# Startup of a one-core diffusion layer: tokens loaded first, the attention modulation in four parts of two k-tiles

## The chip, the cores and the metric

The kernel runs on one core of one Trainium2 chip. The metric is device microseconds of one launch; the median of three runs of the kernel before is 1153.03 us (1152.22 to 1153.11).

## The reference, cut to what matters

The program computes one transformer layer for 512 latent tokens (`x_sample`) and 128 context tokens (`x_prompt`), width 1024, in fp32. The change touches only how it begins:

```python
mod_ctx = (jax.nn.silu(c_ctx) @ w_mod[l] + b_mod[l])[None, None, :]
mod_lat = (jax.nn.silu(c) @ w_mod[l] + b_mod[l])[:, None, :]
...
shift1, scale1, gate1, shift2, scale2, gate2 = jnp.split(mod, 6, axis=-1)
h = rms_norm(x, g_attn) * (1.0 + scale1) + shift1
m, own_ctx = token_mixing(h, mix_w, rope, ctx, lam_init)   # begins with h @ w_in
```

`shift1` and `scale1` are the first 2048 of the 6144 columns of `w_mod` (1024 x 6144). The product `h @ w_in` cannot start before some rows of `h` (transposed: k-tiles of 128 channels) are modulated, and the k-tile k needs columns 128k to 128k+127 of both shift and scale. After it come the two attentions, the output projection and the expert layer of 16 experts, which take the other 1080 us and are not touched.

## The kernel before, in words

The program is written engine by engine, with semaphores; each engine runs its own list in the order in which it is written.

**Loads.** SyncE (SP) issues the weight stream. `STREAM` lists chunks of 1 MB (128 partitions x 2048 floats) and `LOADS` the order of their loads. The first eight chunks, `("part", p, q)`, hold shift and scale columns of the attention modulation: half p of the columns (four k-tiles of shift, four of scale), rows 2q and 2q+1 of the eight k-blocks. Then come the chunks of the dense products, `("gemm", j, q)`. Chunks go round a ring of `NRAW` = 4 buffers `raw`, and a load waits until the chunk four places earlier has been used (`s_half`). The first dense chunk, `FIRST`, has a buffer of its own, `raw_first`, and is loaded between the two halves. After the first part chunk SP also loads `tab` (identity and constants, 100 KB) and five token tiles `x_n` (512 KB each). ScalarE's (ACT's) queue loads the six small rows of `vec` (c, c_ctx, norms, b_mod). GpSimd (POOL) loads `tab2` (rope tables and selectors, 452 KB) at the start, and when part chunk (1, 1) has landed the first key cache, the four lambda rows and two norm rows spread over the partitions (`s_bc`), and the value caches.

**Start.** TensorE (PE) transposes `vec` (L866) after ACT's silu (L1270), and VectorE (DVE) copies it to `vec_t` (L1612). For each token tile, ACT squares and sums it (L1282), POOL takes one over the root (L2232, L2235), DVE scales it (L1654), PE transposes it in 8 pieces (`turn_tokens`, L828), and ACT and DVE copy the two halves out to `x_t` (L1275, L1658). `part_chunk(p, q)` (L807) is four matmuls with 2 stationary columns (c and c_ctx). When a half is complete DVE copies it (`copy_row`, L1620), PE turns it into columns (`part_turn`, L817), and DVE adds the bias (L1625) and forms the scale (L1634). `spin(n)` (L872) is n matmuls of the identity with itself, whose result nobody reads; six more of that kind (L890) follow the first turn.

**First dense product.** `first_step(k)` (L927 to L929) multiplies k-tile k with 512 columns for the five token tiles in banks 0 to 4, three matmuls each: both operands are split into a rounded part (`w_hi`, `ht` high, by ACT, L537 and L1292/L1294) and a rest (`raw_lo`, `ht` low, by DVE, L542 and L1688). Steps 0 to 5 are `first_step`; k-tiles 6 and 7 are the end of `product(0, ...)` (L775 to L777). Between the steps stand the part chunks of half 1 and its turn. Then PE turns the first cached keys (`turn_keys`, L906, copied out by ACT, L1308) and starts `product(1, ...)`. The squares of the first product (L1323) wait in ACT's list behind two splits and an exponential of the lambdas, which wait for DVE.

## Time and profile before

| | |
|---|---|
| median of 3 runs | 1153.03 us |
| profiled execution, first to last instruction (span) | 1148.9 us |
| its own time | not listed apart; the three runs stand 3.3 to 4.2 us above its span |
| PE busy | 1099.2 us (96%) |
| PE's first instruction | 8.67 us |
| first dense matmul | 30.31 us |
| last matmul of the first dense product | 64.7 us |

The span is the time between the first and the last instruction of one profiled execution; what lies around it is launch and completion, so a change of the span is carried over to the median as it is. A busy PE is not a PE at its peak: matmuls are pipelined, and the busy time of a group contains the time that it ran slowly.

### The profile page before, as it was taken

The page shows a single profiled execution, that of the slowest core. Times are in us where ns is not written, and L with a number is a line of the kernel's source. Part 1 is how long each engine was busy: PE and PEld are TensorE (multiplying, and loading weights), DVE is VectorE, ACT ScalarE, POOL GpSimd, SP SyncE. Part 2 cuts the span into 40 slices and gives each one's busy share as a digit, 9 for nine tenths or more (in the row PEclk, how much of TensorE's full clock was granted, in tenths as well). Part 3 has the DMA queues.
Part 4 walks back from the last instruction along what each step waited for, and adds up shares of the span by engine and source line. Part 5 has one row for each costly group of instructions (what it writes and reads, how often), then busy time and mean ns, then how long its engine had stood idle before and what let it go on. Part 6 is the DMA issues. An engine that isn't in the chain of part 4 may idle for free.

```text
span 1148.9 us, 28297 instructions
## 1 busy us (share of the span) xinstructions
PE 1099.2 (96%) x12561; PEld 835.7 (73%) x12561; DVE 543.8 (47%) x993; ACT 369.2 (32%) x856; POOL 154.4 (13%) x213
## 2 busy tenths in 40 slices
PE   6999998999999999999998999999999999999983
PEld 4679887777877777777878777777777777777662
DVE  3575458889968232325877133332233222333235
ACT  4343236777754123122162321222222222211103
POOL 1342440000000000002012111111111111110020
PEclk9999999999999999999999999999999999999996
DMA  9952232212052543368989999999999999999993
GB/s 359 306 224 73 74 74 58 44 25 47 1 198 73 184 146 102 119 220 285 322 301 365 371 403 406 406 406 411 413 407 406 408 406 408 405 408 408 407 322 135
DMA packets 87467, 302.53 MB, mean 263 GB/s; under 512 B 27329, under 2 KB 28610, under 8 KB 62258
## 3 DMA queue, kind: packets, MB, share of 16 engines
q1 hardware_dynamic: 79680, 273.38, 62.0%
q0 software_dynamic: 6528, 20.10, 6.1%
q10 hardware_dynamic: 1138, 7.25, 1.7%
q8 instruction: 99, 1.62, 0.6%
q14 instruction: 22, 0.18, 0.0%
HBM read 276.86 MB, written 18.60 MB: 257 GB/s over the span
## 4 chain that ended last, share of the span: by engine, by line
PE 80%; DVE 6%; DMA 6%; issue 3%; ACT 3%; ACTq 0%; SPq 0%; POOLq 0%; POOL 0%; DVEq 0%
PE ps L1194 39%; PE ps L775 9%; PE ps L777 9%; PE ps L776 9%; PE ps L1001 3%; PE ps L985 2%; DVE neg_max L1794 2%; DMA x_dram<-y_row,rows_t 2%; PE ps L1024 1%; PE ps L1020 1%; DMA x_dram<-xn_p 1%; DVE q_lo_t L1786 1%; PE ps L797 1%; DMA raw<-in_w_in_dram 1%; DMA x_f<-x_dram 1%
## 5 line engine op out<-in xcount | busy, mean ns | idle before, releaser
L2122 DVE SCALAR_TENSOR_TENSOR y_row<-ps,gates,gate_q 32x256 f32<-32x256 f32 (+1 forms) x184 | 88.3, 480 | 237.4 <-PE ps L1194 234.9
L1549 ACT ACTIVATE h_t<-ps 128x256 f32<-128x256 f32 x48 | 15.0, 384 | 371.7 <-PE ps L1194 371.7
L775 PE MATMUL ps<-w_hi,ht 128*128 128x512 f32 (+1 forms) x320 | 124.8, 390 | 0.0
L777 PE MATMUL ps<-w_hi,ht 128*128 128x512 f32 (+1 forms) x320 | 121.8, 381 | 0.0
L776 PE MATMUL ps<-raw_lo,ht 128*128 128x512 f32 (+1 forms) x320 | 121.7, 380 | 0.0
L1194 PE MATMUL ps<-late,xe 128*32 128x256 f32 x1824 | 100.3, 379 | 0.0
L542 DVE TENSOR_TENSOR raw_lo<-raw,w_hi 128x1024 fp32r<-128x1024 f32 x48 | 57.7, 1225 | 78.5 <-ACT w_hi L537 78.0
L1194 PEld LDWEIGHTS ps<-late,xe 128*32 128x32 f32 x1824 | 71.9, 110 | 26.5
L2379 POOL DMA_INDIRECT xg<-x_dram,rows x48 | 46.1, 960 | 318.7 <-PE ps L1194 290.5
L537 ACT ACTIVATE w_hi<-raw 128x1024 fp32r<-128x1024 f32 x48 | 48.8, 1052 | 122.3 <-DMA raw<-in_w_in_dram 67.5
L1539 ACT ACTIVATE xe<-xt,mods_q 128x64 f32<-128x64 f32 x240 | 78.0, 423 | 7.6 <-DVE gates L2106 7.6
L1194 PE MATMUL ps<-raw,xe 128*32 128x256 f32 x1392 | 80.0, 379 | 0.0
L775 PEld LDWEIGHTS ps<-w_hi,ht 128*128 128x128 f32 x320 | 60.1, 188 | 16.6 <-issue 5.2
L1194 PE MATMUL ps<-raw_gate,xe 128*32 128x256 f32 x1248 | 71.3, 379 | 0.0
L1194 PEld LDWEIGHTS ps<-raw,xe 128*32 128x32 f32 x1392 | 54.9, 110 | 20.2
L777 PEld LDWEIGHTS ps<-w_hi,ht 128*128 128x128 f32 x320 | 60.0, 188 | 12.8
L1194 PE MATMUL ps<-late,ht 128*32 128x256 f32 x1200 | 67.5, 379 | 1.1 <-issue 1.1
L776 PEld LDWEIGHTS ps<-raw_lo,ht 128*128 128x128 f32 x320 | 60.2, 188 | 11.3
L1194 PEld LDWEIGHTS ps<-raw_gate,xe 128*32 128x32 f32 x1248 | 49.2, 110 | 18.2
L2113 DVE TENSOR_TENSOR h_t<-h_t,ps 128x256 f32<-128x256 f32 x48 | 19.0, 395 | 88.7 <-PE ps L1194 88.7
L1194 PEld LDWEIGHTS ps<-late,ht 128*32 128x32 f32 x1200 | 47.2, 110 | 18.9 <-issue 1.5
L1794 DVE TENSOR_REDUCE neg_max<-ps 128x1 f32<-128x768 f32 x64 | 58.2, 950 | 2.5 <-PE ps L985 2.4
(325 smaller groups left out, 1916.5 us busy)
## 6 DMA issues: line engine op xcount, KB each, us to landing
late<-in_w_exp_down_dram SPq DMA_DIRECT2D x25, 1024.0 KB, 25.6
late<-in_w_exp_up_dram SPq DMA_DIRECT2D x21, 1024.0 KB, 21.4
late<-in_w_exp_gate_dram SPq DMA_DIRECT2D x17, 1024.0 KB, 23.8
raw<-in_w_in_dram SPq DMA_DIRECT2D x16, 1024.0 KB, 5.8
raw<-in_w_exp_gate_dram SPq DMA_DIRECT2D x16, 1024.0 KB, 23.1
raw_gate<-in_w_exp_up_dram SPq DMA_DIRECT2D x14, 1024.0 KB, 26.4
raw<-in_w_exp_up_dram SPq DMA_DIRECT2D x13, 1024.0 KB, 28.0
raw_gate<-in_w_exp_down_dram SPq DMA_DIRECT2D x13, 1024.0 KB, 24.2
```

The source lines that it names most:

```text
L537: act.activation(w_hi[:, n % NHL, :], raw_half(raw, h), ACT.Copy).then_inc(s_hi, 1)
L542: dve.tensor_tensor(raw_half(raw_lo, h), raw_half(raw, h), w_hi[:, n % NHL, :].bitcast(F32), ALU.subtract)\
L775: pe.matmul(b, stat_hi(k, tt), hi[:, kk, :], start=first, stop=False)
L776: pe.matmul(b, stat_hi(k, tt), lo[:, kk, :], start=False, stop=False)
L777: mm = pe.matmul(b, stat_lo(k, tt), hi[:, kk, :], start=False, stop=last)
L985: mm = pe.matmul(bank(bb, 0, n), q[:, m % 4, t * P:(t + 1) * P], keys_t[:, x, c0:c0 + n], start=(part == 0), stop=(part == 1))
L1001: mm = pe.transpose(bank(4 + n % 3, b * P, (b + 1) * P), prob_row(2 * i + x // per)[:, kt * P:(kt + 1) * P], ident)
L1194: mm = pe.matmul(out[32 * q:32 * q + 32, :], x[:, k, :], columns_of(w, q), start=(k == 0), stop=(k == KD - 1))
L1539: a = act.activation(xe[:, n % 2, sets, k, :], xt[:, sets, k, :], ACT.Identity, scale=mods_q[:, k, v:v + 1], bias=mods_q[:, k, 2 + v:3 + v])
L1794: dve.tensor_reduce(nm, src[:, :, 0:384], AX.XY, ALU.max, negate=True).then_inc(s_max, 1)
L2122: return dve.scalar_tensor_tensor(y_row[n % 2][32 * v:32 * v + count, 256 * q:256 * q + 256], bank(b, o, o + 256, src), gates[src, n % EG, ...
L2379: pool.indirect_dma_start(xg[:, n % 2, v, :], None, x2_quarters[:, :], bass.IndirectOffsetOnAxis(ap=rows[:, v, n:n + 1], axis=0))\
```

## The change

The attention modulation comes in `NPART` = 4 parts instead of two halves. Part p has the columns of k-tiles 2p and 2p+1 (256 of shift, 256 of scale) and two chunks of 1 MB, each with four k-blocks. The number of chunks, their bytes and the ring stay; a row of a part chunk in memory is now 1 KB instead of 2 KB.

- SP loads `tab` and the five token tiles before everything else, then parts 0, `raw_first`, parts 1, 2 and 3, and the second dense chunk.
- ACT squares two token tiles before it waits for `vec` and applies silu, and copies the first transposed tile out before the last square.
- PE transposes all token tiles with only 8 instead of 16 spins ahead and between, and multiplies two part chunks instead of four before the first turn. The chunks of parts 1, 2 and 3 and their turns stand inside `first_step` 0 to 4.
- Parts 1 to 3 use bank 7; each waits for the copy of the part before. Scale and bias are formed for two k-tiles at a time. DVE does the second low split between the copy and the bias of part 1; ACT and DVE take the second chunk's first split after k-tile 4 instead of 3.
- The selector for the turns (`T_SELM`) moves into `tab`. POOL loads `tab2`, the caches and the small rows only when the second dense chunk (`("gemm", 0, 1)`) has landed, and PE waits for `tab2` before `product(3)`.

```diff
-STREAM = [("part", p, q) for p in range(2) for q in range(KD // 2)] + \
+NPART = 4
+STREAM = [("part", p, q) for p in range(NPART) for q in range(2)] + \
...
-PART_BANKS = (0, 7)
+PART_BANKS = (0, 7, 7, 7)
...
-                w = w_mod[0][2 * q * P:(2 * q + 2) * P, 0:2 * D]
-                chunks.append([(slice(0, P), w.rearrange("(k p) (s f n) -> p k s f n", p=P, s=2, f=2)[:, :, :, j, :])])
+                w = w_mod[0][4 * q * P:(4 * q + 4) * P, 0:2 * D]
+                chunks.append([(slice(0, P), w.rearrange("(k p) (s f n) -> p k s f n", p=P, s=2, f=NPART)[:, :, :, j, :])])
...
+            sp.dma_start(tab[:, :], constants[:, 0:T_KEPT]).then_inc(s_tab, 16)
+            for t in range(NT):
+                sp.dma_start(x_n[:, t, :], xs[t] if t < NTL else x_prompt[0]).then_inc(s_x[t], 16)
             for n in LOADS:
...
-                if n == 0:
-                    sp.dma_start(tab[:, :], constants[:, 0:T_KEPT]).then_inc(s_tab, 16)
-                if n == 0:
-                    for t in range(NT):
-                        sp.dma_start(x_n[:, t, :], xs[t] if t < NTL else x_prompt[0]).then_inc(s_x[t], 16)
...
+                if p >= 2 and q == 0:
+                    pe.wait_ge(s_row, p)
+                for g in range(4):
+                    mm = pe.matmul(bank(PART_BANKS[p], rows=slice(32 * g, 32 * g + 2)), c_t[:, 4 * q + g, :],
+                                   raw[:, chunk % NRAW, g * NW:(g + 1) * NW], start=(q == 0), stop=(q == 1))
...
-            part_chunk(0, 0)
-            spin(8)
-            turn_tokens(0)
-            turn_tokens(1)
-            spin(8)
-            part_chunk(0, 1)
-            turn_tokens(2)
-            turn_tokens(3)
-            part_chunk(0, 2)
-            turn_tokens(4)
-            part_chunk(0, 3)
-            pe.wait_ge(s_tab2, 16)
+            spin(4)
+            turn_tokens(0)
+            spin(4)
+            turn_tokens(1)
+            turn_tokens(2)
+            part_chunk(0, 0)
+            turn_tokens(3)
+            turn_tokens(4)
+            part_chunk(0, 1)
             spin(6)
             part_turn(0)
...
-            first_step(0)
-            part_chunk(1, 1)
-            first_step(1)
-            part_chunk(1, 2)
-            part_chunk(1, 3)
-            first_step(2, between=lambda: part_turn(1))
-            first_step(3).then_inc(s_half, 4 // 2)
-            first_step(4)
+            first_step(0, [(2, part_chunks, 1)])
+            first_step(1, [(2, part_turn, 1)])
+            first_step(2, [(2, part_chunks, 2)])
+            first_step(3, [(1, part_turn, 2), (4, part_chunks, 3)]).then_inc(s_half, 2)
+            first_step(4, [(3, part_turn, 3)])
...
-            act.wait_ge(s_vec, 16 * 6)
-            act.activation(vec[0:16, :], vec[0:16, :], ACT.Silu).then_inc(s_actfn, 1)
...
+                if t == 1:
+                    act.wait_ge(s_vec, 16 * 6)
+                    act.activation(vec[0:16, :], vec[0:16, :], ACT.Silu).then_inc(s_actfn, 1)
+                if t == 3:
+                    evict_tokens(0)
...
-                if k in (1, 3, 5):
-                    split_hi(act, SPLITS[(k + 1) // 2])
+                if k in (1, 4, 5):
+                    split_hi(act, SPLITS[(1, 4, 5).index(k) + 1])
...
-                if k == 4:
-                    copy_row(1)
-                    part_bias(1)
-                    part_scale(1)
+                if k in (2, 4, 6):
+                    copy_row(k // 2)
+                    if k == 2:
+                        split_lo(dve, SPLITS[1])
+                    part_bias(k // 2)
+                    part_scale(k // 2)
...
-            second_half = CHUNK["part", 1, 1]
+            second_half = CHUNK["gemm", 0, 1]
             pool.wait_ge(s_raw[second_half % NRAW], raw_count[second_half])
             load_key_cache(0)
+            pool.dma_start(tab2[:, :], constants[:, T_KEPT:T_W]).then_inc(s_tab2, 16)
```

How the instructions stand, place by place. First TensorE's list from its first matmul to the first turn; before:

```order
L866 MATMUL ps<-tab,vec 128x81
L807 MATMUL ps<-raw,vec_t 2x512 x4
L872 MATMUL ps<-tab 128x128 x8
L828 MATMUL ps<-tab,x_n 128x128 x16
L872 MATMUL ps<-tab 128x128 x8
L807 MATMUL ps<-raw,vec_t 2x512 x4
L828 MATMUL ps<-tab,x_n 128x128 x16
L807 MATMUL ps<-raw,vec_t 2x512 x4
L828 MATMUL ps<-tab,x_n 128x128 x8
L807 MATMUL ps<-raw,vec_t 2x512 x4
L872 MATMUL ps<-tab 128x128 x6
L817 MATMUL ps<-tab_74,mod_row 128x4 x4
```

and now (`part_chunk` is L803):

```order
L866 MATMUL ps<-tab,vec 128x81
L872 MATMUL ps<-tab 128x128 x4
L828 MATMUL ps<-tab,x_n 128x128 x8
L872 MATMUL ps<-tab 128x128 x4
L828 MATMUL ps<-tab,x_n 128x128 x16
L803 MATMUL ps<-raw,vec_t 2x512 x4
L828 MATMUL ps<-tab,x_n 128x128 x16
L803 MATMUL ps<-raw,vec_t 2x512 x4
L872 MATMUL ps<-tab 128x128 x6
L817 MATMUL ps<-tab,mod_row 128x2 x4
```

Two part chunks and eight spins are gone from here; the token tiles follow each other more closely. (In the trace a spin or a part matmul counts as two records, a transposed piece as one.)

Second, ScalarE's list from its first function to the first split; before:

```order
L1270 ACT_TABLE_LOAD
L1270 ACTIVATE vec<-vec 16x128
L1282 ACTIVATE squares,ss<-x_n 128x1024 x5
L1275 ACTIVATE x_t<-ps 128x4x128 x5
L537 ACTIVATE w_hi<-raw_first 128x1024
```

and now:

```order
L1275 ACT_TABLE_LOAD
L1275 ACTIVATE squares,ss<-x_n 128x1024 x2
L1278 ACT_TABLE_LOAD
L1278 ACTIVATE vec<-vec 16x128
L1275 ACTIVATE squares,ss<-x_n 128x1024 x2
L1268 ACTIVATE x_t<-ps 128x4x128
L1275 ACTIVATE squares,ss<-x_n 128x1024
L1268 ACTIVATE x_t<-ps 128x4x128 x4
L535 ACTIVATE w_hi<-raw_first 128x1024
```

Silu (L1278) now stands behind two squares, and a second table load has come ahead of it.

Third, VectorE's list around k-tile 2, one piece of the difference:

```order
 L1682 TENSOR_SCALAR h_tmp_65<-x_t,scale,mod_t 128x128
 L1688 TENSOR_TENSOR ht<-h_tmp_65,ht 128x640
-L542 TENSOR_TENSOR raw_first_lo<-raw_first,w_hi 128x1024
+L1618 COPY mod_row<-ps 128x512
+L540 TENSOR_TENSOR raw_first_lo<-raw_first,w_hi 128x1024
+L1623 TENSOR_TENSOR mod_t<-ps,vec_t 128x2x4
+L1632 SCALAR_TENSOR_TENSOR scale<-mod_t,vec_t 128x4
```

K-tile 2 now waits for a copy, a turn on PE, a bias and a scale of its own part, with the second low split between.

## Rows read from the trace of the kernel before

**Rows 1.** the page: span, and the chain that ended last by engine

```profile
span 1148.9 us, 28297 instructions
...
PE 80%; DVE 6%; DMA 6%; issue 3%; ACT 3%; ACTq 0%; SPq 0%; POOLq 0%; POOL 0%; DVEq 0%
```

**Rows 2.** who TensorE waited for, first 70 us: total, times, longest

```profile
PE ps L866 <- ACT vec L1270: 8.7, 1, 8.7
PE ps L927 <- DVE raw_lo L542: 2.0, 1, 2.0
PE ps L906 <- ACT keys_t L1308: 1.0, 1, 1.0
```

**Rows 3.** timeline of TensorE, 0 to 30 us: start, us, what

```profile
9.37 1.89 PE L807 MATMUL ps<-raw,vec_t 128*2 128x512 f32 x8 [0.34 <-DVE vec_t L1612]
11.19 3.79 PE L872 MATMUL ps<-tab 128*128 128x128 f32 x16
14.77 2.16 PE L828 MATMUL ps<-tab,x_n 128*128 128x128 f32 x16
16.77 1.95 PE L872 MATMUL ps<-tab 128*128 128x128 f32 x16
...
25.93 0.95 PE L817 MATMUL ps<-tab,mod_row 128*128 128x4 f32 x8
26.74 1.64 PE L890 MATMUL ps<-w_hi 128*128 128x512 f32 x6
```

**Rows 4.** windows: us, busy PE, PEld, DVE, ACT, POOL; PEclk, DMA, GB/s

```profile
9.00:12.00 3.00, 2.67 (x13) 0.92 (x13) 1.15 (x3) 2.73 (x5) 1.33 (x4) 1.00 1.02 411
```

**Rows 5.** timeline of TensorE, 30 to 65 us, the first dense product

```profile
30.31 0.47 PE L927 MATMUL ps<-w_hi,ht 128*128 128x512 f32 x1 [0.49 <-DVE ht L1688]
...
38.60 1.90 PE L807 MATMUL ps<-raw,vec_t 128*2 128x512 f32 x16
...
50.56 0.50 PE L927 MATMUL ps<-w_hi,ht 128*128 128x512 f32 x1 [2.04 <-DVE raw_lo L542]
...
57.67 0.39 PE L775 MATMUL ps<-w_hi,ht 128*128 128x512 f32 x1
...
64.67 0.38 PE L906 MATMUL ps<-tab,ka_parts 128*128 128x128 f32 x2
```

**Rows 6.** timeline of ScalarE, 0 to 11 us

```profile
3.24 1.28 ACT L1270 ACT_TABLE_LOAD   x1 [3.24 <-issue]
8.22 0.31 ACT L1270 ACTIVATE vec<-vec 16x128 f32<-16x128 f32 x1 [3.70 <-DMA vec<-in_g_diff_norm_dram]
8.85 1.06 ACT L1282 ACTIVATE squares<-x_n 128x1024 f32<-128x1024 f32 x1 [0.33 <-DMA x_n<-in_x_sample_dram]
...
10.13 1.06 ACT L1282 ACTIVATE squares<-x_n 128x1024 f32<-128x1024 f32 x1
```

**Rows 7.** timeline of VectorE, 26 to 57 us

```profile
26.99 0.17 DVE L1625 TENSOR_TENSOR mod_t<-ps,vec_t 128x16 f32<-128x16 f32 x1 [1.60 <-PE ps L817]
...
29.35 0.81 DVE L1688 TENSOR_TENSOR ht<-h_tmp,ht 128x640 fp32r<-128x640 f32 x1
...
55.54 0.83 DVE L1688 TENSOR_TENSOR ht<-h_tmp,ht 128x640 fp32r<-128x640 f32 x1
```

**Rows 8.** landing after issue: first two part loads, last norm row (L2271)

```profile
DMA to landing us min/median/max: 3.8/4.3/4.8
...
DMA to landing us min/median/max: 9.3/9.3/9.3
```

**Rows 9.** DMA packets and SP queue, 48:52 and 50:54 us

```profile
DMA packets 883, 1.52 MB, mean 380 GB/s; under 512 B 30, under 2 KB 264, under 8 KB 883
...
q1 hardware_dynamic: 873, 1.50, 103.2%
...
DMA packets 1126, 1.41 MB, mean 352 GB/s; under 512 B 21, under 2 KB 857, under 8 KB 1126
...
q1 hardware_dynamic: 1126, 1.41, 103.1%
```

More of the change, by code:

```diff
@@ L221, in table_of_constants @@
         t[v::32, T_SELM + v] = 1.0
-        for f in range(2):
-            t[32 * f + v::64, T_SELP + 2 * f + v] = 1.0
         t[v::32, T_SB + v * P:T_SB + (v + 1) * P] = 1.0
@@ L915, in cached_keys, with first_step @@
                     turn_keys(("b", 1, 1))
-            def first_step(k, between=None):
+            def first_step(k, between=()):
                 h = gemm_half(0, k // 2)
@@ L923, in first_step @@
                 for t in range(NT):
-                    if t == 2 and between:
-                        between()
+                    for at_tile, work, p in between:
+                        if t == at_tile:
+                            work(p)
                     b, tt = bank(t), slice(t * P, (t + 1) * P)
@@ L1282, in _ @@
                 act.activation(squares[:, :], x_n[:, t, :], ACT.Square, accum_out=ss[:, t:t + 1]).then_inc(s_ss, 1)
-            for t in range(NT):
+                if t == 1:
[3 more added lines that the diff above has]
+                    evict_tokens(0)
+            for t in range(1, NT):
                 evict_tokens(t)
```

70 lines of the change are left out of this document (32 added, 38 removed).

## The prediction

> **What bounds the kernel now.** I read the page first, then who waited for whom on TensorE, then the engines' timelines for the first 70 us, then the loads. The chain that ended last is 80% TensorE [rows 1], and from 8.67 us on this engine hardly rests. In the first 70 us it waited 8.7 us for `vec`, 2.0 us ahead of dense step 4 (for the split of a chunk that came late), and 1.0 us at the cached keys [rows 2]. Whatever the change gains it must take from these waits, from slow time or from work; the rest of the program follows TensorE and the other engines as they come out of this stretch, so I carry a shift at the start of `product(1)` over to the end.
>
> One thing the busy time hides: the same 16 records of spins take 3.79 us from 11.19 us on and 1.95 us from 16.77 us on [rows 3]. The granted clock already reads 1.00, the upper level of 2.4 GHz, in 9 to 12 us [rows 4], but the records show about half speed until 14.8 us, 5.6 us after the engine began steady work at 9.37 us. The slow stretch holds one part chunk and eight spins.
>
> **Part 1: when TensorE starts.** It waits for silu on `vec`, which ran at 8.22 us after 3.7 us of waiting for the last small row; the only table load, 1.28 us, lay in that wait [rows 6]. Now two squares stand ahead of silu, and a second table load. The first two loads (512 KB each, issued at 0.7 and 1.2 us) landed after 3.8 and 4.8 us [rows 8], so 0.5 MB is there at 4.5 us and 1 MB at 6.0 us. The table and two token tiles are 1.1 MB: estimate 4.8 us for the first, 6.3 us for the second. A square takes 1.28 us from start to start (8.85 to 10.13, [rows 6]), so the second ends at 7.6, the table is in at 8.9, silu is done at 9.2 us instead of 8.53: **+0.65 us**. Bounds: 0 if tokens land early enough for the table load to end before `vec` is there, +1.5 us if the second token comes at 7.2.
> The Trainium skill (ScalarE: Activation LUTs, "What ACT_TABLE_LOAD costs") gives about 1.28 us for the load and 1.38 us of drain with it; by that silu would come 1.4 us later still, and TensorE's start would be late by 2 us. The trace's own load is followed by a wait and cannot show the drain.
>
> **Part 2: to the first dense step.** I keep the slow stretch at 5.6 us from the first spin at 10.0 us. Four spins (1.9 us), one tile of transposes (8 records at twice 0.12, 1.9 us) and four spins (1.9) fill it exactly: 15.6 us. Then four tiles at 0.98 us (two take 1.96 to 2.16, [rows 3]) and two part chunks at 0.95 (16 records in 1.90, [rows 5]) give 21.4. The scaled tokens keep up: VectorE's pieces between two tiles (a copy out and a scaling) are the same as before. Part 0 is 4.7 MB into the queue, about 17 us at the later rates, so it hides behind the transposes. Six spins are 1.5 us, and from the start of the turn to the first dense matmul it was 25.93 to 30.31, 4.4 us [rows 3, 5]: **the dense product starts at 27.2 us, 3.1 us earlier**. What this consists of: two part chunks and eight spins out (1.9 + 1.8 us at full speed), against the later start.
>
> **Part 3: the dense product.** Before, from 30.31 to 64.67, were eight steps (3.5 us each: 57.67 to 64.67 are two), three part chunks, a turn and a wait of 2.04 us [rows 5]. Now there are six chunks (5.7 us), three turns (25.93 to 26.74, 0.81 us each, 2.4), and eight steps (28.0). After a break the first matmul takes 0.50 instead of 0.39 us [rows 5]; six breaks are 0.7 us. Sum 36.8 us.
> A new wait: k-tile 2 needs part 1, whose turn ends 1.4 + 0.8 us into step 1. From the end of a turn to the next k-tile: the bias started 0.25 us later, the low part (without the split of 1.1 us that stood between) would have ended near 29.4 us, 2.7 us after the turn [rows 3, 7]. Step 1 needs only 2.1 us for its last three tiles, so step 2 waits **0.5 us**. Parts 2 and 3 have a step or more of slack. VectorE's second low split lies before the turn and costs nothing; without that cover it would cost 1.2.
> The 2.04 us wait ahead of step 4 goes. `gemm(0, 1)` is issued when part 2 is used, near 41 us, into an empty queue; the 3.8 to 4.8 us of [rows 8] bring it to 46, and step 4 starts near 49.
> Sum: 27.2 + 36.8 + 0.5 = **64.5 us against 64.67**. The 3.1 us are given back: the part chunks are only moved, two turns are new (1.6 us), and what ran in the shadow of the first modulation now runs between dense steps.
>
> **Part 4: what comes behind.** The wait of 1.0 us at the keys hangs on ScalarE and VectorE, whose splits and squares follow the last k-tile, low part done at 56.37 us [rows 7]. Part 3's turn ends 2.9 us into step 4, near 52.6 us; 2.7 us to k-tile 6 and 1.6 to k-tile 7 give 56.9: **+0.5 us**. TensorE's wait for the keys grows by the same and the end moves by +0.5.
>
> **Loads.** A part row is now 1 KB. In 48 to 52 us 609 packets of 2 KB and 264 smaller than that took 103.2% of 16 engines for 4 us (66.0 us), in 50 to 54 us 269 and 857 took 66.0 us [rows 9]; the two give 87 ns for 2 KB and 50 ns for 1 KB. So a part chunk takes 3.2 us instead of 2.8, and eight chunks 3.3 us more. Each has more than that in hand: `raw_first` lands near 20 us, part 1 near 26, wanted at 28.7, part 2 near 33, wanted at 39. Cost nothing, up to 1 us if the queue is slower than I think. POOL issues the small rows from 46 us; the last norm row, 5 us later, took 9.3 us to land [rows 8] and would be there at 60, while VectorE wants it near 61. Nothing, but with 1 us of slack.
>
> **Forecast.** The span goes from 1148.9 to 1149.4 us. The three runs' median, 1153.03, stands 4.1 us above the span, so 1153.5 us. A measurement of this kernel can tell about 0.2%, 2.3 us, from no change.
>
> **Rivals.** (A) **The slow stretch gets longer**, which ends slower. Its place is 12 to 22 us, where transposes and short waits for tokens now follow each other and only eight spins are left. Each tile or part chunk run at half speed costs 1 us more; if all six after 15.6 us do, +5.8 us, and half of them +2.9. It decides once three stay slow. Against it: after 14.8 us the transposes ran fast between part chunks. For it: before, no transpose ran in the stretch ahead of the rise. Times 1156.4 to 1159.3.
> The Trainium skill (TensorE: Matmul & The Clock Gate, "Part 4: PE-mode transpose") says that transposes do not count as activity as matmuls do. By that this rival would be the forecast; the trace so far has matmuls alone ahead of the rise, so it does not settle it.
> (B) **More of the 3.1 us stays**: tokens land by 5.5 us, so the start is not late (-0.65), TensorE becomes fast at 14.8 us as before (-0.4), step 2 does not wait because the low part starts sooner (-0.5), and the low parts of k-tiles 6 and 7 come early enough for the wait at the keys to go (-1.0). Together -2.6 from +0.5: 1151.0 us, and 1150 if ScalarE's splits behind them gain another us; with part of it 1152. Against it: the second table load stands in the list.
> (C) **The small rows come late.** If the last norm row lands after 61 us, VectorE's lambdas, ScalarE's exponential behind them and the squares of the first product all wait, and each us is one for TensorE: +1 to +3, 1155 us. They compete with three dense chunks and the caches.
> (D) The change does not do what it says: the instruction lists show that it does, so I give it nothing.
>
> **Chances.** Forecast 0.55, A 0.14, B 0.24, C 0.07. The likeliest case alone has 1152 to 1155 (start 0 to +1.5, slow stretch 0.8 either way). The range leaves out the outer half of A and the best of B: 1150.6 to 1156.8. Faster by over 0.2%: 0.18, three quarters of B; slower: 0.20, A, half of C and the edge of the forecast's own range; the same 0.62.
>
> **What would show it.** Right: a second table load at about 7.6 us, the transpose of `vec` at 9.2 to 9.4, first dense matmul at 27 us, no wait of 2 us at step 4, a wait near 0.5 at step 2, the last dense matmul at 64 to 65, a wait of 1.5 us at the keys. Spins or transposes at twice their time after 16 us speak for A; a dense start before 26 us for B; a wait of VectorE at L1717 or L1720 for a load, for C. The forecast is wrong if the dense product ends more than 1.5 us from 64.5, or if the shift there does not reach the end.

## The result, and the profile after

The change makes the kernel slower by a little under half a per cent.

| | before | with the change |
|---|---|---|
| median, four runs of each on the same chip | 1152.86 us (1152.22 to 1153.11) | 1158.62 us (1156.51 to 1159.19) |
| ratio, 95% interval | | 1.0044 (1.0030 to 1.0058) |
| profiled execution | span 1148.9 us | 1156.51 us, span 1154.5 us |

The profiled execution of the change is its fastest; the other three lie 2 us and more above it. That of the kernel before was a fast one too. In each run for which both are listed the time stands 1.8 to 2.3 us above the span, so with its span of 1148.9 us it took about 1151 us, less than any timed run of that kernel (their spans are 1149.8 us and more, about 1151 us in the median). Of the 4.1 us between its span and the median, which the text ahead of the prediction and the forecast put down to launch and completion, some 2 us are this. For the forecast, a difference added to the median, it makes no odds; the two profiled executions, each some 2 us below its kernel's median, can be compared. The 5.8 us between the medians are more than a measurement can mistake, and the forecast of 1153.5 us, and its upper bound of 1156.8 us, were too low.

The trace of the change follows in the order of the program. ScalarE's timeline shows the start as forecast (columns as in [rows 6]):

```profile
3.02 1.28 ACT L1275 ACT_TABLE_LOAD   x1 [3.02 <-issue]
5.25 1.06 ACT L1275 ACTIVATE squares<-x_n 128x1024 f32<-128x1024 f32 x1 [0.94 <-DMA x_n<-in_x_sample_dram]
...
7.66 1.28 ACT L1278 ACT_TABLE_LOAD   x1
8.96 0.31 ACT L1278 ACTIVATE vec<-vec 16x128 f32<-16x128 f32 x1
```

The second table load stands at 7.66 us (forecast: about 7.6), and silu follows 0.02 us after its end. Next, TensorE's timeline up to the first dense matmul:

```profile
9.41 0.37 PE L866 MATMUL ps<-tab,vec 81*128 81x81 f32 x1 [9.41 <-ACT vec L1278]
10.12 2.08 PE L872 MATMUL ps<-tab 128*128 128x128 f32 x8 [0.34 <-DVE vec_t L1610]
11.99 1.91 PE L828 MATMUL ps<-tab,x_n 128*128 128x128 f32 x8
13.69 1.30 PE L872 MATMUL ps<-tab 128*128 128x128 f32 x8
14.84 1.91 PE L828 MATMUL ps<-tab,x_n 128*128 128x128 f32 x16
...
22.82 1.64 PE L887 MATMUL ps<-w_hi 128*128 128x512 f32 x6
26.33 0.47 PE L924 MATMUL ps<-w_hi,ht 128*128 128x512 f32 x1 [1.86 <-DVE ht L1688]
```

Eight transposes took 1.91 us at 11.99 us, and from 14.84 us on sixteen take the same time: the slow stretch is no longer than before. (Its length differs between executions of the same instructions: the sixteen records of spins at the start took 3.79 us in the kernel before [rows 3], and 3.28, 2.80 and 3.30 us in versions 4, 8 and 9 below, whose start is the same.) The dense product starts at 26.33 us, 0.9 us ahead of the forecast. Ahead of it TensorE pauses for 1.86 us. Who TensorE waited for in the first 75 us (total, times, longest), to be read against [rows 2]:

```profile
PE ps L866 <- ACT vec L1278: 9.4, 1, 9.4
PE ps L924 <- DVE ht L1688: 2.4, 2, 1.9
PE ps L902 <- ACT keys_t L1306: 2.2, 1, 2.2
PE ps L817 <- DVE mod_row L1618: 0.4, 1, 0.4
...
PE ps L771 <- DVE ht L1688: 0.3, 1, 0.3
```

The 2.0 us ahead of step 4 are gone. The wait ahead of step 0 was 0.49 us and is 1.86. New are 0.5 us at step 2 (the second of the two waits in the second row, as forecast), 0.4 us at the last turn and 0.3 us at k-tile 7; the wait at the keys has doubled. TensorE's timeline at the keys and behind them:

```profile
64.95 0.38 PE L902 MATMUL ps<-tab,ka_parts 128*128 128x128 f32 x2
65.17 0.60 PE L902 MATMUL ps<-tab,kb_parts 128*128 128x128 f32 x4
67.95 0.63 PE L902 MATMUL ps<-tab,kb_parts 128*128 128x128 f32 x4 [2.18 <-ACT keys_t L1306]
68.33 0.48 PE L771 MATMUL ps<-w_hi,ht 128*128 128x512 f32 x1
...
68.91 0.63 PE L773 MATMUL ps<-w_hi,ht 128*128 128x512 f32 x1
69.34 0.63 PE L771 MATMUL ps<-w_hi,ht 128*128 128x512 f32 x1
...
71.90 0.55 PE L771 MATMUL ps<-w_hi,ht 128*128 128x512 f32 x1
72.29 0.39 PE L772 MATMUL ps<-raw_lo,ht 128*128 128x512 f32 x1
```

and the windows of the same stretch (busy time by engine, then the granted clock, the DMA share and GB/s):

```profile
69.00:70.00 1.00, 1.00 (x4) 0.80 (x3) 0.46 (x1) 0.21 (x1) 0.83 (x3) 0.50 1.22 512
...
71.00:72.00 1.00, 1.00 (x4) 0.76 (x3) 0.47 (x1) 0.98 (x2) 0.83 (x3) 0.50 1.08 459
```

The first dense product ends at 64.95 us against 64.67 before: still the forecast, to 0.5 us. Then come the two things that were not in it. The third turn of keys starts 1.4 us later than before (at 67.95 us against 66.52; [rows 2] has the wait there before). And right behind the pause the granted clock reads 0.50, the lower level of 1.2 GHz: from 68.9 to 72.3 us a matmul comes every 0.43 us instead of every 0.23, which is about 3.4 us x (1 - 0.23/0.43) = 1.6 us lost. Together 3.0 us, and the attention's scores do start 3.0 us later (176.8 us against 173.8), as does the expert layer 450 us further on (628.5 against 625.5).

Why the keys wait longer is in VectorE's and POOL's timelines ahead of them:

```profile
52.83 0.33 DVE L1632 SCALAR_TENSOR_TENSOR scale<-mod_t,vec_t 128x4 f32<-128x4 f32 x1
53.20 0.76 DVE L1680 TENSOR_SCALAR h_tmp<-x_t,scale,mod_t 128x512 f32<-128x512 f32 x1
53.88 0.41 DVE L1682 TENSOR_SCALAR h_tmp<-x_t,scale,mod_t 128x128 f32<-128x128 f32 x1
54.50 1.22 DVE L1688 TENSOR_TENSOR ht<-h_tmp,ht 128x640 fp32r<-128x640 f32 x1 [0.20 <-ACT ht L1292]
...
56.97 0.83 DVE L1688 TENSOR_TENSOR ht<-h_tmp,ht 128x640 fp32r<-128x640 f32 x1
```

```profile
52.83 0.30 POOL L2248 CAST ka_parts<-k_cache 128x128 fp32r<-128x128 f32 x1
...
56.05 0.80 POOL L2250 TENSOR_TENSOR kb_parts<-k_cache,kb_parts 128x256 fp32r<-128x256 f32 x1
```

POOL now splits the cached keys from 52.8 to 56.9 us, in exactly the stretch in which VectorE makes the last two k-tiles. VectorE's operations grow there: 0.33 us for a scale that takes 0.16 elsewhere, 1.22 us for a low part of 0.83. The last low part ends at 57.80 us instead of the forecast 56.9, and from that end to the third turn of keys it is 10.15 us in both kernels (57.80 to 67.95, and 56.37 to 66.52 before). What lies between is one chain: ScalarE issues the stores of `ht` and splits the next weights, VectorE splits their rest and works on the lambdas, and the squares of the first product follow.

One more loss shows in the profiled execution. The first expert matmuls take 3.59 us at the start, where before they took 1.93 (first row of the change, second of the kernel before, TensorE's timelines):

```profile
628.50 3.59 PE L1189 MATMUL ps<-early,xe 128*32 128x256 f32 x32 [1.70 <-ACT xe L1554]
```

```profile
625.51 1.93 PE L1194 MATMUL ps<-early,xe 128*32 128x256 f32 x32 [1.08 <-ACT xe L1556]
```

That is 1.7 us, again at a granted clock near 0.50 and behind a pause. A further 1.2 us are lost by 681 us, 0.8 us of it in an idle just ahead of 666.07 us that the trace puts down to nothing. From there the distance is 5.9 us, and it is 6.0 us at a landmark late in the experts, the matmul behind a pause of 1.0 us (1088.63 us in the change, 1082.61 us before). At the end it is 5.6 us: the last 30 us hang on loads and VectorE as well as on TensorE, and there the kernel before alone waits 3.03 us for a weight (until 1120.84 us), with half speed behind it. The code of the experts is the same in both kernels.

### The profile page after: what moved, and what is told of

Same layout as the page of the kernel before. It is cut to its first block, busy times and chain, and to the rows that moved or that the text cites. A ratio compares the mean times of both kernels' runs of the same rounds, so it can differ in the third digit from the quotient of the medians.

```text
span 1154.5 us, 28303 instructions
## 1 busy us (share of the span) xinstructions
PE 1100.0 (95%) x12561; PEld 857.0 (74%) x12561; DVE 547.6 (47%) x999; ACT 370.6 (32%) x857; POOL 155.8 (13%) x213
## 4 chain that ended last, share of the span: by engine, by line
PE 80%; DVE 7%; DMA 6%; ACT 3%; issue 3%; ACTq 0%; SPq 0%; POOLq 0%; POOL 0%; DVEq 0%
PE ps L1189 39%; PE ps L771 9%; PE ps L773 9%; PE ps L772 9%; PE ps L996 2%; PE ps L980 2%; DVE neg_max L1792 2%; DMA x_dram<-y_row,rows_t 2%; PE ps L1019 1%; PE ps L1015 1%; DMA x_dram<-xn_p 1%; DMA x_f<-x_dram 1%; DVE q_lo_t L1784 1%; PE ps L793 1%; DVE y_row L2120 1%
## 5 line engine op out<-in xcount | busy, mean ns | idle before, releaser
L1189 PE MATMUL ps<-late,xe 128*32 128x256 f32 x1824 | 103.6, 379 | 0.0
L540 DVE TENSOR_TENSOR raw_lo<-raw,w_hi 128x1024 fp32r<-128x1024 f32 x48 | 57.9, 1228 | 80.2 <-ACT w_hi L535 79.6
L1189 PEld LDWEIGHTS ps<-late,xe 128*32 128x32 f32 x1824 | 78.8, 110 | 21.7
L1189 PE MATMUL ps<-raw,xe 128*32 128x256 f32 x1392 | 86.9, 379 | 0.2
L1189 PE MATMUL ps<-raw_gate,xe 128*32 128x256 f32 x1248 | 77.2, 379 | 0.0
L1189 PEld LDWEIGHTS ps<-raw,xe 128*32 128x32 f32 x1392 | 61.4, 110 | 18.9 <-issue 1.8
L1189 PE MATMUL ps<-late,ht 128*32 128x256 f32 x1200 | 71.8, 379 | 1.0 <-issue 1.0
L1189 PEld LDWEIGHTS ps<-raw_gate,xe 128*32 128x32 f32 x1248 | 55.5, 110 | 15.5
L1189 PEld LDWEIGHTS ps<-late,ht 128*32 128x32 f32 x1200 | 52.3, 110 | 16.5 <-issue 1.7
```

The costliest lines, as they stand in the source:

```text
L540: dve.tensor_tensor(raw_half(raw_lo, h), raw_half(raw, h), w_hi[:, n % NHL, :].bitcast(F32), ALU.subtract)\
L1189: mm = pe.matmul(out[32 * q:32 * q + 32, :], x[:, k, :], columns_of(w, q), start=(k == 0), stop=(k == KD - 1))
```

## The experiments

All medians in this table were taken against the kernel before on the same chip (1152.7 to 1153.4 us there). "Scores" is the first score matmul in the profiled execution, 173.8 us before and 176.8 us with the change.

| version | median (spread, runs), us | ratio to before, 95% | scores, us |
|---|---|---|---|
| change, caches early again (1) | 1159.27 (1157.45 to 1160.84, 5) | 1.0050 (1.0036 to 1.0064) | 180.1 |
| change, spins at the keys (2) | 1157.16 (1155.69 to 1158.54, 5) | 1.0036 (1.0023 to 1.0050) | 177.5 |
| change, one table load (3) | 1155.45 (1154.69 to 1157.84, 11) | 1.0022 (1.0013 to 1.0031) | 176.0 |
| before, caches late (4) | 1150.05 (1149.59 to 1152.8, 8) | 0.9978 (0.9968 to 0.9989) | 170.9 |
| change, pause before step 0 filled (5) | 1156.52 (1155.66 to 1157.44, 6) | 1.0032 (1.0019 to 1.0044) | 177.1 |
| change, POOL waits (6) | 1156.06 (1154.38 to 1158.6, 9) | 1.0026 (1.0016 to 1.0036) | 177.2 |
| change, 3, 5, 6 and four spins (7) | 1154.82 (1153.29 to 1157.48, 11) | 1.0021 (1.0012 to 1.0030) | 173.7 |
| before, caches late, POOL waits (8) | 1149.76 (1149.12 to 1151.79, 11) | 0.9976 (0.9967 to 0.9985) | 170.3 |
| 8 without the six idle matmuls (9) | 1152.74 (1150.97 to 1155.06, 11) | 0.9992 (0.9983 to 1.0001) | 173.3 |
| change, vectors first again (10) | 1158.49 (1155.6 to 1159.49, 5) | 1.0043 (1.0029 to 1.0057) | 177.0 |

Two versions, 4 and 8, are faster than both kernels; version 9 can't be told from the kernel before. The versions of the change spread by 2 to 4 us from run to run, so a difference of 1 to 2 us between two of them is weak evidence by itself; where I lean on one, it is together with the trace. The profiled execution is the slowest of its version in 1 and 9, and the fastest in 7.

**1. Caches early again.** In the change:

```diff
-second_half = CHUNK["gemm", 0, 1]
+second_half = CHUNK["part", 1, 1]
```

> The change, but POOL again issues the caches, tab2 and small rows when part chunk (1, 1) has landed instead of the second dense chunk. Theory 1 (POOL's splitting of the cached keys, moved to 53 to 57 us, stretched VectorE's low parts of k-tiles 6 and 7 by 1.3 us; TensorE's wait at the keys grew to 2.2 us and after it the granted clock was 0.50 for 3.4 us): POOL's key parts move to about 30 to 36 us, L1688 of the last two k-tiles is back at 0.83 us, the wait at the keys is 1.2 us or less, the clock stays at 1.00 in 68 to 72 us, and the span is 2 to 3 us shorter than the change's 1154.5 (part of it may come back where the later low stretch of the clock falls). Theory 2 (the new waits on the parts' own chain are the cause, POOL is innocent): no change at 57 us, the wait at the keys stays at 2.2. Theory 3 (bandwidth: early caches push parts 2 and 3 back): TensorE waits for raw<-in_w_mod ahead of parts 2 or 3 and the span is 1 to 3 us longer.

VectorE's low parts are back at 0.83 us and the wait at the keys is down to 0.4 us, as the first theory has it. But the time does not fall: the ratio, 1.0050, can't be told from the change's 1.0044. TensorE's waits in the first 80 us:

```profile
...
PE ps L924 <- DVE raw_lo L540: 2.5, 1, 2.5
...
PE ps L902 <- ACT keys_t L1306: 0.4, 1, 0.4
```

The wait ahead of step 4 has come back, at 2.5 us: with POOL's loads running, the second dense chunk is late. So POOL's work costs something wherever it is put: early it delays a chunk, late it delays VectorE. This execution also started 0.7 us later, as its first token landed late (first square at 5.96 us instead of 5.25), its first stretch at half speed lasted longer, so that the dense product started 1.7 us later than in the change (28.00 us), and behind the 2.5 us TensorE ran at half speed: the turn at 56.62 us took 1.87 us instead of 0.95.

**2. Spins at the keys.** In the change, between the second and the third key turn:

```diff
             turn_keys(("b", 0, 0))
+            for _ in range(8):
+                pe.matmul(bank(5, 0, P), ident, ident, start=True, stop=True)
             turn_keys(("b", 0, 1))
```

> The change with eight spins (16 records, 1.9 us) into the empty bank 5 between the second and the third turn of the cached keys, where TensorE waits 2.2 us. Theory 1 (the idle at the keys is what the lower clock follows): product(1) starts at the same time, within 0.2 us, the granted clock stays at 1.00 in 68 to 72 us, and the shift of everything behind is 1.5 us smaller (attention scores from 175.3 instead of 176.8). Rival (the lower clock comes at that time whatever the engine does): clock 0.6 in 68 to 72 us all the same, scores from 176.8.

At the keys the expectation holds: the wait behind the spins is 0.3 us and the granted clock stays at 1.00 from 66 to 74 us. The time, 1157.2 us, is only 1.5 us better (by the ratios 0.9 us, with overlapping intervals). In the profiled execution the scores come 0.7 us later than in the change, not 1.5 us earlier. Its second token landed late, so its dense product started 0.5 us later; most of the rest shows in TensorE's timeline and in the windows:

```profile
26.82 0.48 PE L924 MATMUL ps<-w_hi,ht 128*128 128x512 f32 x1 [1.87 <-DVE ht L1690]
...
28.62 3.28 PE L803 MATMUL ps<-raw,vec_t 128*2 128x512 f32 x16
```

```profile
28.00:30.00 2.00, 2.00 (x10) 0.27 (x13) 0.25 (x1) 0.00 (x0) 0.00 (x0) 0.51 1.08 346
30.00:32.00 2.00, 2.00 (x13) 0.33 (x6) 0.03 (x1) 0.00 (x0) 0.00 (x0) 0.64 0.41 117
```

The pause of 1.87 us ahead of step 0 is followed by half speed too: 3.28 us for the part chunks that take 1.90 in the change's own trace. There the same pause (1.86 us) passed without it, as it did in the profiled executions of 1, 3, 6 and 10 (1.86 or 1.87 us): one of six had the lower clock. That may be a part of the spread of the change's runs; the traces, one for each version, don't show how large a part.

**3. One table load.** In the change, a silu of one element ahead of the squares:

```diff
+            act.wait_ge(s_dve, 1)
+            act.activation(q_sq[0:1, 0, 0:1], bank(0, 0, 1, slice(0, 1)), ACT.Silu)
             end_b = HALVES_B
```

> The change with one silu of a single element (result unused) ahead of the squares, so that the table that holds both functions is loaded first and only once. If the second table load delays the start, the transpose of vec begins 0.7 to 1.2 us earlier (8.2 to 8.7 instead of 9.4) and the first dense matmul 0.4 to 0.7 us earlier than 26.3; the last small row of vec is the next thing late. Whether that reaches the end: theory 1 expects VectorE's contention with POOL to stay as long as the second dense chunk lands when part 2's use lets it be issued, so 0.5 us at the keys. Rival: vec lands at 9 us anyway, nothing moves.

The one load, at 3.03 us, serves both functions; silu comes at 7.97 us, TensorE starts at 8.41 us and the dense product at 25.64. At 176.0 us the scores are 0.8 us earlier than in the change. The median is 3.2 us lower (by the ratios 2.5 us, with intervals that overlap by a hair), more than the trace explains: the pause at the keys, 2.2 us, and half speed behind it are still there.

**4. The kernel before with the caches late.** The reverse of experiment 1, in the kernel before:

```diff
-second_half = CHUNK["part", 1, 1]
+second_half = CHUNK["gemm", 0, 1]
```

> The kernel before, with one edit of the change alone: POOL issues the caches and small rows when the second dense chunk has landed (46.3 us) instead of part chunk (1, 1). Theory 1: POOL's key parts fall on 53 to 57 us, L1688 of the last two k-tiles takes up to 1.2 us, VectorE's last low part ends about 1.3 us later than 56.4, TensorE's wait at the keys is about 2.3 us instead of 1.0, and if the clock follows it 1.5 us more are lost: span +1.3 to +3. Theory 2 (POOL is innocent): within 0.3 us of the kernel before up to 80 us. Should the lambda rows land too late, VectorE waits at L1719 or L1722 and that is a third cause.

This is 2.7 us faster than the kernel before (2.5 us by the ratio). TensorE's waits in the first 80 us, against [rows 2]:

```profile
PE ps L866 <- ACT vec L1270: 8.7, 1, 8.7
PE ps L906 <- ACT keys_t L1308: 1.0, 1, 1.0
PE ps L807 <- DMA raw<-in_w_mod_dram: 1.0, 1, 1.0
...
```

The 2.04 us ahead of step 4 are gone. ScalarE's timelines of the second dense chunk's first split say why, in this version and then in the kernel before:

```profile
40.23 1.06 ACT L537 ACTIVATE w_hi<-raw 128x1024 fp32r<-128x1024 f32 x1 [7.96 <-DMA raw<-in_w_in_dram]
```

```profile
46.30 1.06 ACT L537 ACTIVATE w_hi<-raw 128x1024 fp32r<-128x1024 f32 x1 [13.39 <-DMA raw<-in_w_in_dram]
```

The chunk lands 6 us sooner when POOL's loads do not run beside it; SyncE issued it at 34.42 us here and at 35.06 us in the kernel before, so 5.4 us of the 6 are its own way. My first theory for this run, a longer wait at the keys, fell: VectorE's low parts are stretched as it says (to 1.39 us), but the wait is 1.04 us as before, because the dense product and the low parts both end earlier.

At the scores this trace is 2.9 us ahead (170.9 against 173.8). The one line is worth 2.3 us of them, by which the dense product is shorter (from 34.36 to 32.06 us). The other 0.6 us stand already at the first dense matmul (29.67 against 30.31), before the edit can act, where this execution had the shorter slow stretch at the start. All the rest of the change costs 5.9 us at the scores, by these two traces.

**5. The pause before step 0 filled.** In the change, 13 instead of 6 of the idle matmuls behind the first turn.

```diff
-            for _ in range(6):
+            for _ in range(13):
                 pe.matmul(bank(1), w_hi[:, 0, 0:P], w_hi[:, 0, 0:NW], start=True, stop=True)
```

> The change with 13 instead of 6 idle matmuls (L887) after the first turn, so that TensorE does not stand still for 1.9 us ahead of the first dense step. Theory 1 (after a pause of about 2 us the granted clock is sometimes 0.50 for 3.4 us; in the run with spins at the keys that stretch fell on 28 to 31 us and cost the chunks of part 1 1.4 us): step 0 starts at the same distance from the first turn, the clock stays at 1.00 in 26 to 32 us in every execution, and the median comes down by 0.5 to 1.5 us from 1158.6; the keys are untouched. Rival (the pause ahead of step 0 has no part in it): median 1158.6, spread as before.

Step 0 starts at 26.66 us behind a wait of 0.27 us, with the granted clock at 1.00 from 26 to 32 us; at the keys (2.4 us) the clock still falls to 0.50. The median is 2.1 us lower than the change's (by the ratios 1.4 us, with overlapping intervals), and the runs lie within 1.8 us. The profiled execution of the change did not have the slow stretch here, so its scores (176.8 us) are not later than these (177.1). That fits a gain in those executions alone that do have it, but doesn't show it.

**6. POOL waits for the last low part.** In the change:

```diff
             pool.wait_ge(s_kc[0], 32)
+            pool.wait_ge(s_htl, KD)
             make_cached_parts(0)
```

> The change with one wait more on POOL: it splits the first cached keys only when VectorE's eight low parts are done. Theory 1 (POOL's work stretches VectorE's): L1688 of k-tiles 6 and 7 takes 0.83 us and the other rows between them are as short as for k-tile 2, the last low part ends 1.2 us earlier relative to part 3's turn, the wait at the keys is 1.0 to 1.4 instead of 2.2 us; if the clock then stays up in 68 to 72 us the span is 2.5 us shorter, if not 1.2. Rival (VectorE is slow there for another reason, the loads for instance): L1688 stays at 1.2.

VectorE's timeline of the last two k-tiles, against the block of the change above:

```profile
53.52 0.16 DVE L1632 SCALAR_TENSOR_TENSOR scale<-mod_t,vec_t 128x4 f32<-128x4 f32 x1
...
55.02 0.83 DVE L1688 TENSOR_TENSOR ht<-h_tmp,ht 128x640 fp32r<-128x640 f32 x1 [0.50 <-ACT ht L1292]
```

So it was POOL's splitting that stretched VectorE's operations: with it out of the way, the bias of the last part (52.63 us in the change, 53.31 here) is 5.17 us from the end of the last low part in the change and 4.11 us here. But the wait at the keys stayed, at 2.46 us. TensorE too was quicker, 37.95 us from the first dense matmul to the keys instead of 38.62, and the chain from the last low part to the third turn grew from 10.15 to 10.98 us: POOL's splitting now lies beside VectorE's next operations, the splits of the dense chunks. Two of them (L540) take 2.84 us here, from 60.10 us on, instead of 2.36 in the change, from 60.13. That is 0.5 us of the 0.8; the rest lies ahead of ScalarE's splits, where the issue of two stores of `ht` took 1.51 us instead of 1.16. The contention is moved, not gone.

**7. Four repairs together.** The edits of 3, 5 and 6, and four spins at the keys instead of the eight of 2.

> The change with four repairs together: one table load, 13 idle matmuls ahead of step 0, POOL behind the low parts, four spins between the key turns. If the losses are these pauses and what the clock does after them: start 8.4, first dense matmul 25.6, keys done at 65.5, clock 1.00 to 600 us; 1153 to 1154.5 us, that is no better than the kernel before, since four parts cost two turns more. If a further cause is hidden in the four parts it stays above 1155.

The clock reads 1.00 in every window from 26 to 76 us, and the scores start at 173.7 us, 3.1 us earlier than in the change: all that the trace of the change had lost up to there. The wait at the keys beyond the four spins is still 1.5 us. It brings the layer of four parts level with the kernel before, not ahead of it, and the median, 1154.8 us, is still 2 us above. In the traces these 2 us come up at the experts: at their first matmul this version is 0.6 us ahead (624.91 against 625.51), and at the landmark of 1082.61 us it is 2.2 us behind. Versions 4 and 8 lose there too, from 2.7 and 3.1 us ahead to 0.2 and 1.2 us ahead, and their code there is that of the kernel before. So this loss is not the four parts'; the profiled execution of the kernel before had an unusually quick passage there.

**8. The best version.** The edit of 4 and that of 6, in the kernel before.

> The kernel before with caches and small rows issued when the second dense chunk has landed, and POOL's split of the keys behind the low parts. The late issue alone gave 1150.05 us, although L1688 was stretched to 1.39 us. Theory 1: the low parts of k-tiles 6 and 7 end 0.8 to 1 us earlier, the wait of 1.04 us at the keys shrinks by that, 1149.2 us. If the wait moves to POOL's parts instead, 1150.

1149.76 us, ratio 0.9976 (0.9967 to 0.9985), against the change's 1.0044: it is the fastest of all. The low part that POOL had stretched to 1.39 us in version 4 is back at 0.83, the wait at the keys is 0.40 us instead of 1.04. Against version 4 this is 0.6 us at the scores, and 0.3 us in the medians, which they cannot tell from nothing.

**9. A pause made on purpose.** Version 8 without the six idle matmuls (L890), which change nothing but how long TensorE stands still:

```diff
-            for _ in range(6):
-                pe.matmul(bank(1), w_hi[:, 0, 0:P], w_hi[:, 0, 0:NW], start=True, stop=True)
```

> This is the fastest version so far (kernel before, late caches, POOL's key splitting after the low parts) without the six idle matmuls (L890) ahead of part chunk (1, 0). They ran from 27.09 us after a wait of 1.51 us and took 1.65 us, and after them the chunk and step 0 follow at 28.71 and 29.68 at full speed. Theory 1 (a pause of about 2 us or more is followed by some 3.4 us at the lower level of the clock): the pause grows to about 3 us unless the chunk and k-tile 0 are ready sooner; granted clock near 0.50 in two or three of the microseconds after 28 to 29 us, 16 dense records in about 3.3 us instead of 1.9, scores 1.5 us later than 170.3 us, about 1151.3 us. Theory 2 (a pause costs only its own length): part chunk (1, 0) and step 0 start at the same time or earlier, the clock stays at 1.00, 1149.8 us or a few tenths less.

TensorE's timeline behind the first turn, first in version 8 and then in this one, and two of its windows:

```profile
27.09 1.65 PE L890 MATMUL ps<-w_hi 128*128 128x512 f32 x6 [1.51 <-ACT w_hi L537]
28.71 1.04 PE L807 MATMUL ps<-raw,vec_t 128*2 128x512 f32 x8
```

```profile
29.34 1.89 PE L807 MATMUL ps<-raw,vec_t 128*2 128x512 f32 x8 [2.98 <-DMA raw<-in_w_mod_dram]
31.16 0.80 PE L925 MATMUL ps<-w_hi,ht 128*128 128x512 f32 x1
31.75 0.63 PE L926 MATMUL ps<-raw_first_lo,ht 128*128 128x512 f32 x1
...
34.31 0.48 PE L926 MATMUL ps<-raw_first_lo,ht 128*128 128x512 f32 x1
34.63 0.39 PE L927 MATMUL ps<-w_hi,ht 128*128 128x512 f32 x1
```

```profile
28.00:29.00 1.00, 0.00 (x0) 0.00 (x0) 1.00 (x2) 1.00 (x3) 0.00 (x0) 0.50 1.05 387
...
33.00:34.00 1.00, 1.00 (x4) 0.77 (x3) 0.97 (x3) 0.00 (x0) 0.00 (x0) 0.50 1.05 387
```

Leaving out work that nobody reads makes the kernel slower: the scores come 3.0 us later (173.3 against 170.3), and the ratio to the kernel before goes from 0.9976 (0.9967 to 0.9985) to 0.9992 (0.9983 to 1.0001), some 1.8 us. The clock falls while the engine stands still, at about 27.7 us, and stays at 0.50 for 6.8 us. Of the 3.0 us, 0.6 are the part chunk, which landed later here (29.34 us against 28.71 at the latest); from its start to the keys it is 35.39 us instead of 33.03, and these 2.4 us are what half speed costs. My expectation had the direction, and 1.5 us. The profiled execution is the slowest of eleven, so the median of 1.8 us is the better size for the whole. Theory 2, that a pause costs only its own length, falls.

**10. Vectors first again.** In the change, the order of loads, of ScalarE's first operations and of TensorE up to the first turn as in the kernel before; the four parts and the late caches stay.

```diff
-            sp.dma_start(tab[:, :], constants[:, 0:T_KEPT]).then_inc(s_tab, 16)
-            for t in range(NT):
-                sp.dma_start(x_n[:, t, :], xs[t] if t < NTL else x_prompt[0]).then_inc(s_x[t], 16)
             for n in LOADS:
...
-            spin(4)
+            part_chunk(0, 0)
+            spin(8)
             turn_tokens(0)
-            spin(4)
             turn_tokens(1)
+            spin(8)
+            part_chunk(0, 1)
             turn_tokens(2)
-            part_chunk(0, 0)
             turn_tokens(3)
             turn_tokens(4)
-            part_chunk(0, 1)
...
+            act.wait_ge(s_vec, 16 * 6)
+            act.activation(vec[0:16, :], vec[0:16, :], ACT.Silu).then_inc(s_actfn, 1)
...
-                if t == 1:
-                    act.wait_ge(s_vec, 16 * 6)
-                    act.activation(vec[0:16, :], vec[0:16, :], ACT.Silu).then_inc(s_actfn, 1)
```

> This is the change with the order of the start taken back: the first part chunk loads ahead of the constants and tokens, silu stands ahead of the squares (one table load), and TensorE multiplies part chunk (0, 0), spins 8, turns tokens 0 and 1, spins 8, multiplies (0, 1) and turns tokens 2 to 4. The four parts and the late caches stay. Theory 1 (the late and scattered start is one of several causes, the rest sits in the pauses before step 0 and at the keys): first TensorE instruction at 8.5 us, first dense matmul near 26.5 us, waits of 0.3 to 0.5 us inside the dense steps and 2 us at the keys as in the change, scores at 175 to 176.5 us, 1155 to 1157 us. Theory 2 (loading tokens first is the whole cost, the four parts are harmless): about the 1150 us of the kernel before with late caches, scores near 171 us. Theory 3 (the token order does not matter): as the change, 1158.6 us, scores at 176.8 us.

The median is the change's (1158.49 against 1158.62). TensorE starts 2.0 us earlier (7.46 us), but reaches the dense product 1.3 us later than in the change:

```profile
27.67 0.47 PE L925 MATMUL ps<-w_hi,ht 128*128 128x512 f32 x1 [1.87 <-DVE ht L1688]
```

Loading the tokens first, then, is not what costs; by this trace it gains 1.3 us at the dense product. The scores are nearly level all the same (177.0 us against 176.8): here the wait at the keys was 2.60 us, and the granted clock stayed at 1.00 behind it. From the first dense matmul to the keys it is 38.65 us here and 38.62 in the change, against 32.06 in version 4. What is left of the change beside it is the four parts, and the cost is there. Of the three theories the third came nearest in time, though not for its reason.

**The account.** Version 4 differs from the change in everything but the late caches. From it to the change, by the traces:

| term | us |
|---|---|
| dense product starts (29.67, now 26.33) | -3.34 |
| from there to the keys (32.06, now 38.62) | +6.56 |
| wait at the keys (1.04, now 2.18) | +1.14 |
| lower clock behind it | +1.6 |
| sum; the scores say 176.8 - 170.9 | +6.0; +5.9 |

The 6.56 us are three more part chunks inside the product (2.9 us, six times 0.95 against three), two more turns (1.6), waits of 0.52, 0.37 and 0.25 us (1.1), and about 0.9 us of breaks, by subtraction. The first row has the luck of two executions in it, since the slow stretch at the start differs by up to 1 us.

## Why the prediction was wrong

**Part 1 was right.** Second table load at 7.66 us, TensorE at 9.41 us, as forecast. The drain that the Trainium skill names (ScalarE: Activation LUTs, "What ACT_TABLE_LOAD costs") does not show: silu followed the load after 0.02 us. In experiments 1, 2 and 6 a token landed late (the first, the second, and both) and the start came at 10.1 to 10.2 us, at the bound of +1.5 that I had given for it.

**Part 2 was right but for its rest.** 26.33 us instead of 27.2, so 0.9 us better. That is the slow stretch, over by 14.84 us instead of 15.6, and it is luck: in experiment 1 it lasted longer, and from TensorE's first matmul to the dense product it was 17.9 us, as the forecast has it (9.3 to 27.2), and not 16.9. (From 9.37 to 14.8 us it is 5.4 us, not the 5.6 that I wrote.) I also carried the 4.4 us from the turn to the first dense matmul over as they were, without asking what TensorE does in them. Before, part chunk (1, 0) stood there for 1.04 us, with waits of 0.40 us ahead of it and 0.49 us behind it [rows 5]:

```profile
28.78 1.04 PE L807 MATMUL ps<-raw,vec_t 128*2 128x512 f32 x8 [0.40 <-DMA raw<-in_w_mod_dram]
```

The change takes the chunk out, VectorE is no faster, and one pause of 1.86 us is left.

**Part 3 was right.** The product took 38.6 us against 36.8 + 0.5, for the waits of 0.37 and 0.25 us at part 3 and k-tile 7, where I had given a step or more of slack, and breaks a little longer than counted; with the start 0.9 us early, the end at 64.95 met 64.5. The wait of 0.5 us at step 2 measured 0.52. That the wait ahead of step 4 goes was right, and its reason wrong: I put it on an empty queue at a later issue. Experiment 4 shows that in the kernel before it hung on POOL's loads beside the chunk; with these moved it goes without any part of the rest.

**Part 4 is the step that failed: "+0.5 us" at the keys and "I carry a shift ... over to the end".** It is two errors, and the second is the larger. The first is one of size: the last low part ended 1.4 us later than before instead of 0.5, and the wait grew by 1.14 us, because POOL's splitting of the keys now falls on VectorE's last two k-tiles. That it stretches them, experiment 6 shows; moved behind them it lengthened the chain to the keys instead, and the wait stayed (2.46 us). I had checked the moved loads for their landing ("Loads: cost nothing") and forgotten the work that POOL does when they have landed. The second is one of kind: I priced each pause at its own length. A pause of about 2 us can have a price behind it, at the lower level of the clock: 1.6 us at the keys in the profiled execution, 1.4 us at step 0 in experiment 2, and 2.4 us in experiment 9 behind a pause of 2.98 us. My sum had nothing for it. Nor does the end simply follow `product(1)`: a shift of 3.0 us there became 5.9 us at the experts and 5.6 us at the end.

**The rivals.** A had the right mechanism, a stretch at half speed that costs some us, and its time range holds the result, by luck; its place was wrong. It put the stretch at 12 to 22 us, among the transposes, and there the trace is as before. By the rule of the Trainium skill that I set beside it (TensorE: Matmul & The Clock Gate, "Part 4: PE-mode transpose") the transposes should have kept the clock down; sixteen of them from 14.84 us on ran in 1.91 us, so this case does not show it. B: one of its four gains came, TensorE fast by 14.8 us (worth 0.8 us here), and the pauses ate it; the start was late, step 2 waited, and the wait at the keys grew. C: VectorE never waited for a load at L1717 or L1720. The rival that I did not have was that one half of the change gains (version 4, -2.7 us) and the other loses about three times that.

**What stays open.** The change's median lies 5.8 us above the kernel before, and 3.0 us are accounted for up to the scores. In the profiled executions nearly all the rest comes up in the first 60 us of the experts. 1.7 us of it are half speed at their first matmuls. The change and experiments 1, 2, 3, 5, 6, 9 and 10 have it, behind pauses of 1.3 to 3.2 us; the kernel before and versions 4, 7 and 8 passed the same place at full speed, 4 and 8 behind pauses of 1.8 and 1.7 us. Why the change should meet it is not shown, and no version fills this pause. But versions 4 and 8 lose about as much on the kernel before there, 2.5 and 1.9 us from the first expert matmul to the landmark of 1082.61 us, at full speed. Against version 4, whose profiled execution took its median time, the change is 5.9 us behind at the scores, 5.7 at the first expert matmul, 6.2 at that landmark and 6.6 at the end. So most of what seems lost at the experts is the quick passage of that one execution of the kernel before. What the traces don't show is why the change's median lies 2.1 us above its profiled execution. The executions in which the pause ahead of step 0 is followed by the lower clock may be a part of it: experiments 3 and 5 have lower medians without a matching shift in their traces, and a time alone doesn't tell which executions those were.

## What to carry to other kernels

Price a pause of the matrix engine by what follows it, not only by its length: look at the granted clock and at the matmuls' spacing for a few microseconds behind each wait of a microsecond and more, and try idle matmuls where a wait can't be removed. When loads are moved, follow also the work that starts when they land, on whichever engine, and the transfer that used to run beside them. And test the parts of a change apart: here one line gained 0.2%, and everything else around it lost 0.7%. And compare a profiled execution's own time with the median before reading differences of a microsecond or two from it: here that of the kernel before was 2 us quicker than its median.

## What the runs showed of the hardware

- **The clock behind a pause.** At the keys, pauses of 2.18 to 2.46 us were followed by a granted clock of 0.50 for about 3.4 us (the change, experiments 3, 5 and 6), and one of 2.60 us was not (experiment 10). Behind the pause of 1.86 or 1.87 us ahead of step 0 it fell in one profiled execution (experiment 2) and not in five. In experiment 9 it fell during the pause of 2.98 us and stayed down for 6.8 us. So length alone doesn't decide it, and these runs don't say what does.
- **POOL beside VectorE.** While POOL casts and subtracts tiles of 128x128 and 128x256, VectorE's subtraction of 128x640 took 1.22 us (change) and 1.39 us (version 4) instead of 0.83. With POOL's work moved away it was back at 0.83 (experiments 6 and 8).
- **Small loads beside a large one.** With POOL's loads beside it, the second dense chunk could be split 11.2 us after its issue (35.06 to 46.30 us, the kernel before), without them 5.8 us after it (34.42 to 40.23 us, version 4).
